# Near-head bias tables from one raw table per head, the zeroing of a scratch array later in the load queue, and an input scaling that strides its writes

## The reference, cut to what matters

```python
def modulate(h, shift, scale):
    return rms_norm(h) * (1 + scale) + shift

# neighbourhood attention, for one grid row r
rpb_cols = rpb[:, :, col_idx - cols[:, None] + (NA_COLS - 1)]
bias = jnp.take(rpb_cols, r0 + jnp.arange(wr) - r + (NA_ROWS - 1), axis=1)
s_loc = einsum("bhqd,bhrqwd->bhqrw", q_r, k_nb) * scale + transpose(bias)
s_ctx = einsum("bhqd,bhkd->bhqk", q_r, k_ctx) * scale
p = softmax(concatenate([s_loc, s_ctx]))

# expert layer
a = gelu(einsum("thkd,td->thk", u_emb[e], xb))
return einsum("thk,thkd->td", g * a, v_emb[e])
```

## Time and profile before

| | us |
|---|---|
| median of three runs | 3447.33 (3445.88 to 3447.69) |
| the profiled execution | 3442.6 |
| its span, first to last instruction | 3440.5 |
| busy: PE / DVE / POOL / ACT | 3297.2 / 2183.3 / 1837.6 / 1083.2 |
| mean granted clock | 0.979 |

### The profile page before, as it was taken

The page is one execution under the profiler, slowest core; times in us unless marked ns, Lnnn a source line. Parts: engine busy times, 40 slices in busy tenths (PEclk is TensorE's granted clock), DMA queues, the critical chain, the costliest instruction groups (busy, mean ns, idle before and its releaser), DMA issues.

```text
span 3440.5 us, 45632 instructions
## 1 busy us (share of the span) xinstructions
PE 3297.2 (96%) x17004; PEld 2879.3 (84%) x17004; DVE 2183.3 (63%) x4167; ACT 1083.2 (31%) x1491; POOL 1837.6 (53%) x1166
## 2 busy tenths in 40 slices
PE   7998379999999999999999999999999999999999
PEld 3886257888878888999999778888888888999998
DVE  7877342488745422899998341688555323999997
ACT  3226244233334322222222333233334322222222
POOL 0000014347788861877772463357888752777761
PEclk9999689999999999999999999999999999999999
DMA  7772521146988894999998122255669865999995
GB/s 283 265 258 57 191 80 71 49 141 155 244 229 167 173 251 148 366 361 357 384 359 301 62 74 86 89 142 143 144 147 177 181 164 206 370 362 360 359 361 214
DMA packets 569952, 733.82 MB, mean 213 GB/s; under 512 B 272130, under 2 KB 404867, under 8 KB 553092
## 3 DMA queue, kind: packets, MB, share of 16 engines
q1 hardware_dynamic: 414084, 529.10, 47.5%
q0 software_dynamic: 118784, 134.68, 15.2%
q10 hardware_dynamic: 36864, 67.13, 5.4%
HBM read 610.92 MB, written 119.80 MB: 212 GB/s over the span
## 4 chain that ended last, share of the span: by engine, by line
PE 89%; SPq 5%; DVE 3%; DMA 1%; issue 1%; ACT 1%; DVEq 0%; ACTq 0%
PE ps L1508 41%; PE ps L1553 30%; PE ps L1468 5%; PE ps L1417 4%; PE ps L1280 4%; SPq L746 3%; SPq L728 1%; PE ps L1528 1%; PE ps L1458 1%; DVE macc L1793 1%; DMA modall<-in_w_mod 0%; DVE xm L1772 0%; PE ps L1232 0%; PE ps L1406 0%; SPq L739 0%
## 5 line engine op out<-in xcount | busy, mean ns | idle before, releaser
L1642 POOL DMA_INDIRECT G_scratch<-pick,gidx x512 | 887.0, 1732 | 283.1 <-issue 211.1
L1508 PE MATMUL ps<-xhi,Uhi 128*128 128x512 f32 x2048 | 801.0, 391 | 2.4 <-DVE Ulo L1992 2.4
L1508 PE MATMUL ps<-xhi,Ulo 128*128 128x512 f32 x2048 | 797.7, 390 | 0.0
L1508 PE MATMUL ps<-xlo,Uhi 128*128 128x512 f32 x2048 | 797.1, 389 | 0.0
L1553 PE MATMUL ps<-Hhi,Vhi 128*128 128x384 f32 x2048 | 686.0, 335 | 3.7 <-DVE Hlo L2202 3.7
L1553 PE MATMUL ps<-Hlo,Vhi 128*128 128x384 f32 x2048 | 684.7, 334 | 0.0
L1553 PE MATMUL ps<-Hhi,Vlo 128*128 128x384 f32 x2048 | 684.7, 334 | 0.0
L1992 DVE TENSOR_TENSOR Ulo<-Uraw,Uhi 128x1024 fp32r<-128x1024 f32 x230 | 281.8, 1226 | 578.9 <-ACT Uhi L1070 577.5
L1133 ACT CAST Vhi<-Vraw 128x1024 fp32r<-128x1024 f32 x256 | 269.9, 1054 | 779.6 <-PE ps L1553 764.6
L1649 POOL DMA_INDIRECT picked<-act_scratch,aidx x256 | 381.5, 1490 | 229.6 <-DMA act_scratch<-act_st 152.2
L1508 PEld LDWEIGHTS ps<-xhi,Uhi 128*128 128x128 f32 x2048 | 384.7, 188 | 81.3 <-DVE Ulo L1992 2.9
(11 more groups left out here) (297 smaller groups left out, 3979.2 us busy)
## 6 DMA issues: line engine op xcount, KB each, us to landing
Uraw<-in_UT SPq DMA_DIRECT2D x128, 1024.0 KB
Vraw<-in_V SPq DMA_DIRECT2D x256, 512.0 KB, 5.5
act_scratch<-act_st ACTq DMA_DIRECT2D x256, 256.0 KB
act<-act_scratch SPq DMA_DIRECT2D x256, 192.0 KB, 5.6
modw<-in_w_mod SPq DMA_DIRECT2D x80, 512.0 KB, 4.7
G_scratch<-zeros SPq DMA_DIRECT2D x32, 1024.0 KB, 10.2
Gin<-G_scratch SPq DMA_DIRECT2D x256, 128.0 KB
ring<-in_query SPq DMA_DIRECT2D x8, 2048.0 KB, 8.0
```

The costliest lines, as they stand in the source:

```text
L1508: mm = nc.tensor.matmul(up_bank(m), w, x[:, k, :], start=(k == 0 and j == 0), stop=(k == KT - 1 and j == 2))
L1642: nc.gpsimd.indirect_dma_start(G_dram[layer].rearrange("m p (t o) -> (m p t) o", o=1), bass.IndirectOffsetOnAxis(ap=gidx[r][:, h * TOPK + ...
```

## The change

There are three parts. (1) `braw` holds one raw table of 32 key columns per head of the pair, taken from band 1, for all bands; band 0 reads it 8 columns further on (`TABLE_PARTS` (0, 8, 32, 0), with the mask moved back by 8). A near head has 16 loads (8 r by 2), and the masks are 3 loads whose source repeats each row 8 times. `masked_bias` waits for the new counts and has the same instructions. (2) The 16 zeroing DMAs of layer 0 are issued after the last query weight and before the loads of U. (3) In `scaled(0)` the reads are in order and the write steps by 8 elements (32 bytes), 64 at a time.

```diff
--- before.py
+++ after.py
@@ -81,7 +81,7 @@
 TABLE_BANDS = (0, 1, 3)
 TABLE_AT = [sum(NEAR_W[j] for j in TABLE_BANDS[:n]) for n in range(len(TABLE_BANDS) + 1)]
 MASK_AT = [at // NA_ROWS for at in TABLE_AT]
-TABLE_PARTS = (((0, 0, 24, 0), (1, 8, 32, 0)), ((1, 0, 8, 24), (2, 8, 24, 0), (2, 0, 8, 16)))
+TABLE_PARTS = (((0, 8, 32, 0), (1, 8, 32, 0)), ((1, 0, 8, 24), (2, 8, 24, 0), (2, 0, 8, 16)))
 NEAR_KEYS = (((0, 192),), ((128, 320), (64, 128)), ((256, 448), (192, 256)), ((384, 512), (320, 384)))
 SIDE_AT = (P, P, P, DH)
 
@@ -176,7 +176,7 @@
         oT = sb("oT", 24, [P, KT, T])
         btab = [sb(f"btab{n}", at, [P, 2, TABLE_AT[-1]]) for n, at in enumerate((40, 174))]
         vmix = [sb(f"vmix{n}", at, [P, CW]) for n, at in enumerate((202, 204))]
-        braw = [sb(f"braw{n}", at, [P, 2, TABLE_AT[-1]]) for n, at in enumerate((45, 168.5))]
+        braw = [sb(f"braw{n}", at, [P, 2, NEAR_W[1]]) for n, at in enumerate((45, 168.5))]
         osq = sb("osq", 54, [P, 2, P])
         rspread = sb("rspread", 166, [P, T])
         oms = sb("oms", 168, [P, 2, HA * TT])
@@ -735,29 +735,25 @@
                     sp.wait_ge(bias_masked, h - 1)
                 if h == 0:
                     for n, j in enumerate(TABLE_BANDS):
-                        for r in range(NA_ROWS):
-                            sp.dma_start(mask[r:P:NA_ROWS, MASK_AT[n]:MASK_AT[n + 1]],
-                                         a["mask"][j * BAND:(j + 1) * BAND, BANDS[j][0]:BANDS[j][1]]
-                                         ).then_inc(bias_in[0], 16)
+                        c0, c1 = BANDS[j]
+                        sp.dma_start(mask[:, MASK_AT[n]:MASK_AT[n + 1]],
+                                     a["mask"][j * BAND:(j + 1) * BAND, c0:c1].unsqueeze(1).to_broadcast(
+                                         [BAND, NA_ROWS, c1 - c0])).then_inc(bias_in[0], 16)
                 for r in range(NA_ROWS):
-                    for n, j in enumerate(TABLE_BANDS):
-                        c0, c1 = BANDS[j]
-                        for m in range(2):
-                            sp.dma_start(
-                                braw[h % 2][r:P:NA_ROWS, m, TABLE_AT[n]:TABLE_AT[n + 1]].rearrange(
-                                    "q (s k) -> q s k", s=NA_ROWS),
-                                a["btab"][2 * h + m, j * BAND:(j + 1) * BAND,
-                                          NA_ROWS - 1 - r:2 * NA_ROWS - 1 - r, c0:c1]).then_inc(bias_in[h % 2], 16)
-                if h == 1:
-                    sp.wait_ge(zeros_ready, 1)
-                    for n in range(NZERO):
-                        zero_gates(0, n)
+                    for m in range(2):
+                        sp.dma_start(
+                            braw[h % 2][r:P:NA_ROWS, m, :].rearrange("q (s k) -> q s k", s=NA_ROWS),
+                            a["btab"][2 * h + m, BAND:2 * BAND, NA_ROWS - 1 - r:2 * NA_ROWS - 1 - r,
+                                      BANDS[1][0]:BANDS[1][1]]).then_inc(bias_in[h % 2], 16)
             sp.wait_ge(mix_used, 1)
             load_chunk(W_Q0 + 2)
             load_chunk(W_Q0 + 3)
             sp.dma_start(keysT[:, :, :], a["keysT"][0]).then_inc(keys_in, 16)
             load_chunk(W_Q0)
             load_chunk(W_Q0 + 1)
+            sp.wait_ge(zeros_ready, 1)
+            for n in range(NZERO):
+                zero_gates(0, n)
 
             def load_V(layer, m):
 
@@ -1768,7 +1764,8 @@
                     scale = fing[:, k:k + 1] if sc is None else mods[:, layer, sc + k, who:who + 1]
                     to, rows, roots_of = dst[:, k, :], src[:, k, :], inv
                     if n == 0:
-                        to, rows, roots_of = by_column(to), by_row(rows), by_row(inv)
+                        to = to.rearrange("p (c r) -> p r c", r=NA_ROWS)
+                        rows, roots_of = (x.rearrange("p (r c) -> p r c", r=NA_ROWS) for x in (rows, inv))
                     nc.vector.scalar_tensor_tensor(out=to, in0=rows, scalar=scale,
                                                    in1=roots_of, op0=ALU.mult, op1=ALU.mult).then_inc(x_scaled, 1)
                     if split and k >= 1:
@@ -1857,15 +1854,16 @@
 
             def masked_bias(h, part):
                 if part == 0:
-                    dve.wait_ge(bias_in[h % 2], 16 * NA_ROWS * len(TABLE_BANDS) * (2 * (h // 2 + 1) + 1 - h % 2))
+                    dve.wait_ge(bias_in[h % 2], 16 * (2 * NA_ROWS * (h // 2 + 1) + (0 if h % 2 else len(TABLE_BANDS))))
                 if h == 0 and part == 0:
                     step(nc.vector.tensor_scalar(mask[:, :], mask[:, :], 1.0 / QK_SCALE, None, ALU.mult))
                 for n, c0, c1, to in TABLE_PARTS[part % 2]:
                     rows = slice(TABLE_AT[n], TABLE_AT[n + 1])
+                    reach = mask[:, MASK_AT[n] + c0 - (8 if n == 0 else 0):MASK_AT[n] + c1 - (8 if n == 0 else 0)]
                     last = nc.vector.scalar_tensor_tensor(
                         out=by_column(btab[h % 2][:, part // 2, rows])[:, to:to + c1 - c0, :],
-                        in0=by_row(braw[h % 2][:, part // 2, rows])[:, c0:c1, :], scalar=1.0 / QK_SCALE,
-                        in1=mask[:, MASK_AT[n] + c0:MASK_AT[n] + c1].unsqueeze(2).to_broadcast([P, c1 - c0, NA_ROWS]),
+                        in0=by_row(braw[h % 2][:, part // 2, :])[:, c0:c1, :], scalar=1.0 / QK_SCALE,
+                        in1=reach.unsqueeze(2).to_broadcast([P, c1 - c0, NA_ROWS]),
                         op0=ALU.mult, op1=ALU.add)
                 if part < TT - 1:
                     step(last)
```

## The result

Measured in alternation on one chip: the changed kernel 3360.48 us (median of 4 runs, 3360.14 to 3362.52), the kernel before 3446.61 (4 runs, 3445.07 to 3447.69). The ratio is 0.9752, 95% interval 0.9735 to 0.9769. The profiled execution of the changed kernel took 3360.14 us with a span of 3358.2, which is 82.3 less than the span before.

What follows compares the result with a forecast made beforehand. SP's issuing of many small DMAs was taken to pace the mixer for some 140 us. Terms -73.7 - 2.4 + 2 - 2.5 = -76.6 took the median 3447.3 to 3370.7 us, range 3363 to 3387.

Steps and rivals of the forecast that it cites:

- -73.7: Near heads: DVE's three waits for tables before masking (9.79, 52.99 and 10.91 us) all go.
- Rivals 2, 3 and 4: Table late, 3414 us (0.04); clock low through near heads, 3394 us (0.04); zeroing delays U, 3454 us (0.02).
- The clock behind the stalls: Mixer: DVE's waits for PE at low clock after the stalls shrink, -2.4 us, between 0 and -3.4.
- The cover of the stalls: Mixer: ACT and PE work hidden inside DVE's long wait gets exposed, +2 us, between 0 and +6.
- Rival 1: Mixer: the three stalls covered more work than thought, each removal exposing 3 to 4 us, +10, 3381 us; chance 0.10.
- The masking, priced at nothing: Near heads on DVE: the same 40 masking instructions of the same sizes, so no change in time.
- The scaling: Input scaling on DVE: 4.2 us saved by ordered reads and strided write, of which -2.5 us reaches the projections' start.
- The sign of being wrong that was named for it: Input scaling: eight scalings at 8 us would show that the strided write is not free.
- a bound of PE's: Before the projections: PE works without a gap on the modulation until 45.58, so their start moves by at most -2.5 us.
- my reading of L1977: Strided read plus write there cost 0.34 us more; 0.28 given to the read left 0.06 for the write, nearly free.
- The zeroing "only because it has left this place too": Near heads: head 2's table is in time, 8 us to spare, only with the zeroing moved; otherwise 38 us come first.

Runs made afterwards that it cites:

- tables_only: The change without its zeroing and scaling parts, so only the new table and mask loads and masking, against the kernel before: 3365.94 us, ratio 0.9768.
- filled stalls: The kernel before with extra unread products on PE during its three table waits, in two versions, one with more products: ratios 1.0013 and 0.9994.
- before_again: The kernel before, run again unchanged: 3445.52 us, ratio 0.9997.
- pad40: The changed kernel with raw table rows 160 bytes apart in place of 128: one run, 3396.47 us.
- ladder: The changed kernel with its eight input scalings in eight different access patterns, so its output is another function's: one run, 3379.14 us.
- scale_only: The kernel before with only the input scaling changed to ordered reads and a strided write: 3443.65 us, ratio 0.9996.
- zero_only: The kernel before with only the zeroing moved behind the query weights, 216 small loads kept: 3406.71 us, ratio 0.9894.
- zero_ahead: The changed kernel with the 16 zeroing transfers ahead of the last two query weights in SP's queue: 3421.73 us, ratio 0.9871.

## Why the forecast missed

**What held.** The bound was SP's issuing, in number of transfers: masks and tables went from 15.14 + 64.64 us to 2.15 + 20.5 for the first two heads (the second number from `tables_only`, 0.64 us a load, forecast 0.67; masks 0.72 each, forecast 0.67). It is not the number of pieces inside a transfer either: an old mask load of 16 pieces took 0.63 us, a table load of 128 pieces 0.67. The three waits of the earlier trace rows are gone, so **-73.7** is right to the tenth. The zeroing costs nothing that a trace shows behind the query weights, and runs where it was foretold. Rivals 2, 3 and 4 did not come: no table late, the clock 1.00 from 350 to 390 in the profiled execution (dips to 0.78 to 0.87 in others, which cost 1.5 to 3 us and not 23), and PE's idle time before L1504 3.0 us in the whole execution. The query weights' first load is issued at 410.6, foretold near 416.

**What failed.** The 10.2 us are two things. The profile pair differs by 82.3 us in span where the sum had 76.6: 5.7, which are terms of the sum that were mis-sized. And I carried the 4.7 us between the median before and its profiled execution over to the changed kernel, whose median lies 0.3 above its own: 4.4. That step had no ground: the profiled execution is one of the runs, and in the four later groups that of the changed kernel lay from 13 us below its median to 11.5 above. Here it was bad luck.

In the sum, the part that was mis-sized most is the mixer without its waits for tables: forecast -0.4 (-2.4 and +2), measured -6.1. That is 5.7 too little; the start gave 1.5 where 2.5 was forecast, and everything behind the mixer 1.0 where nothing was, which cancel.

- *The clock behind the stalls, -2.4 forecast.* The step that failed is the wait of 1.03 us at 451.76 taken as what is left "with little changed in the clock". It stands behind the third stall, and the window at 440 of the kernel before shows 0.55 (row below). The three waits (1.44 + 1.98 + 1.03) became 0.57: 3.9 us, above the term's upper bound of 3.4. The filled stalls show that these waits are the clock's. Between the first stall and head 2 it can be added up: 18.04 us became 16.16, of which the clock alone gives 1.4 to 1.5 (16.57 and 16.61 with the stall filled), and the rest, 0.4, is near the masking's 0.5. At the entry of the differential heads the clock dips in both kernels, one group of eight score products apart, which is 1.1 us to the changed kernel's favour in this pair of traces. That is chance: `before_again` enters without a dip, 3.1 us faster than the first trace.

```profile
440.00:450.00 10.00, 4.01 (x32) 3.51 (x34) 5.91 (x18) 1.64 (x4) 0.00 (x0) 0.55 0.06 9
```

- *The cover of the stalls, +2 forecast.* One new wait of 0.56 us for ACT (346.52 above). Rival 1 had the same sign and was further off.
- *The masking, priced at nothing.* It has the same 40 instructions, but not the same rows: 128 bytes apart in place of 96, 2.1 us less of DVE. Between head 1 and head 2 half of such a difference arrives by `pad40` and most of it by the sum above; how much of the whole does is not settled.
- *The scaling, -2.5 forecast.* 9.93 us became 7.86: 2.07 saved in place of the 4.2 worked out, and all of it arrives at the step before the projections (49.23 to 47.17). The sign of being wrong that was named for it, eight scalings at 8 us, came; that the term is off by only 0.4 is luck, since a bound of PE's, which never came to bear, had cut the 4.2 to 2.5. The mixer's start came only 1.5 us earlier in this pair, but on average it lies at 256.4 us in the 12 traces with the new scaling and at 258.8 in the 7 with the old, so the gain lasts. The step that failed is the difference of two rows halved: one strided read was taken as half of two, 0.28. The ladder gives 0.34 for the first strided read and 0.23 for the second, so two reads became one write at the dearer price. The Trainium skill's rule on lines of 16 bytes ("SBUF — State Buffer", "Door 1: The DMA port swizzle") had the write paying like a read and 1.8 us; the ladder agrees (1124 against 1094 ns), and it was nearer than my reading of L1977.
- *The zeroing "only because it has left this place too".* Wrong: `tables_only` has no late table with the zeroing left where it was. I had added its 38 us to a queue that stands idle from 281 to 326; the prediction's own numbers, 283 and 327.8, leave 45 us there.

**How firm is the 6.1?** The stretch between the two loads, without waits for tables, is 159.2, 158.1 and 160.4 us in three traces with the mixer of the kernel before (the third is `scale_only`), and 163.3 in `zero_only`. With PE's clock held up in part by extra products it is 156.9 and 158.5. In five traces of the changed kernel it is 153.1, 154.6, 156.2, 154.2 and 156.9. The mean of the first three is 4.2 above that of the five, so some 2 of the 6.1 us are the luck of the changed kernel's first trace, the shortest of its five, and some 4 stay, ten times the 0.4 forecast. The total moves more: before minus after is 86.1, 84.7, 72.5, 79.2 and 79.7 us on the five chips, against a forecast of 76.6; on four of the five it lies above the forecast. The mechanism and its main term are settled; a range whose lower end allowed 4 us for such waits was too narrow for a kernel whose runs alone spread over 12 us on one chip (3438.8 to 3450.87) and over almost 25 on another (3444.38 to 3469.16).

## What to carry to other kernels

When a queue's timeline is back to back at a low DMA share, count its transfers, not its bytes, and then look where the queue will wait next: a step that was expensive in the queue may be free at the same place once the rest is short. A DMA's slack ends at the first instruction that waits for it in an engine's order, and all that stands behind that instruction waits too; in `zero_ahead` this was a cast on ACT, long before the product that uses the data. And never take a wait as a baseline without reading the granted clock of its own window.

## What the runs showed that I had not expected

- A strided write costs DVE nothing at a step of 8 bytes (746 ns against 751 for 512 elements); one strided operand takes nearly the same from 16 to 256 bytes (1069 to 1133 ns); a second strided read adds 0.23 us. The Trainium skill's page "SBUF — State Buffer", section "Door 1: The DMA port swizzle", says that one can stride four fp32 elements for free and also that a line needs two hits; the rows at 16 bytes bear out the second alone.
- In the masking the row distance matters: 616, 486 and 522 ns at 96, 128 and 160 bytes.
- PE's clock dips in the near heads with PE busy 8 of 10 us (0.73 to 0.87), at different places in different executions. From head 2's masking to DVE's asking for head 3's table the changed kernel takes 19.98 us where there is no dip and 21.57 and 23.06 in two traces with one. Extra products removed the loss of clock at the heads' end on three chips; inside the heads they lifted it behind the stalls, and a dip came elsewhere.
